# One fused program of a hybrid block and a sparse-attention block on one core: index scores gathered first, the choice of keys spread at one round a step, eight heads computed between projections, rotary angles made in the second feed-forward block

## What is computed

```
q = _rope(_rmsnorm(q, q_norm_g), positions)
k = _rope(_rmsnorm(k, k_norm_g), positions)
qi = _rope(qi, positions)
ki = _rope(_layernorm(ki, idx_k_ln_g, idx_k_ln_b)[:, :, None, :], positions)[:, :, 0, :]
...
s = jnp.einsum('bqhd,bsd->bqhs', qib, ki)
score = jnp.einsum('bqhs,bqh->bqs', jax.nn.relu(s), wib).astype(jnp.float32)
score = jnp.where(causal[None], score, -jnp.inf)
_, sel = lax.top_k(score, topk)
...
logits = jnp.where(sel_ok[:, :, None, None, :], logits, -1e30)
p = jax.nn.softmax(logits, axis=-1).astype(vg.dtype)
```

## Time and profile before

| | |
|---|---|
| median of 3 runs | 2787.43 us (2785.8 to 2787.84) |
| the profiled execution's own time | 2788.58 us |
| its span, first to last instruction | 2786.8 us |
| PE busy | 2720.8 us (98%) |
| DVE busy | 1319.9 us (47%) |
| ACT busy | 929.2 us (33%) |
| POOL busy | 757.6 us (27%) |
| mean granted TensorE clock | 0.986 |
| the sparse mixer up to its output projection | about 1553 to 1821 us of the span |

### The profile page before, as it was taken

One profiled execution on the slowest core, in us unless ns is written; L12 is line 12 of the kernel. 1 busy time (PEld: TensorE's weight loads), 2 busy tenths in 40 slices (PEclk: granted clock), 3 DMA queues, 4 the chain that ended last, 5 costly groups with the idle time before them and its releaser, 6 DMA issues.

```text
span 2786.8 us, 30690 instructions
## 1 busy us (share of the span) xinstructions
PE 2720.8 (98%) x12730; PEld 2190.0 (79%) x12730; DVE 1319.9 (47%) x1846; ACT 929.2 (33%) x1505; POOL 757.6 (27%) x627
## 2 busy tenths in 40 slices
PE   7999999999999999999999998999999999999999
PEld 6888886777777777888888765788888888888887
DVE  4343255555656544634434698463332454633323
ACT  4222233333444332432223433643222332332221
POOL 5574015544555476356700231000000000000000
PEclk9999999999999999999999997999999999999999
DMA  5454234333344255344543110023334323333332
GB/s 170 144 148 126 94 109 120 100 91 91 101 115 113 80 144 157 112 135 141 149 130 115 50 53 25 37 68 99 92 99 135 114 75 92 115 104 99 96 115 77
DMA packets 380763, 294.53 MB, mean 106 GB/s; under 512 B 14804, under 2 KB 334544, under 8 KB 380624
## 3 DMA queue, kind: packets, MB, share of 16 engines
q1 hardware_dynamic: 363632, 240.33, 29.3%
q0 software_dynamic: 16992, 52.25, 6.3%
HBM read 290.40 MB, written 2.13 MB: 105 GB/s over the span
## 4 chain that ended last, share of the span: by engine, by line
PE 86%; DVE 8%; ACT 3%; POOL 1%; DMA 1%; issue 1%; SPq 0%; DVEq 0%; ACTq 0%; POOLq 0%
PE PS L361 17%; PE PS L362 17%; PE PS L364 15%; PE PS L433 7%; PE PS L432 7%; PE PS L431 7%; PE PS L366 2%; PE PS L894 1%; PE PS L398 1%; PE PS L399 1%; PE PS L400 1%; PE PS L867 1%; DVE WL L1509 1%; PE PS L564 1%; DVE SCW L2112 1%; PE PS L589 1%
## 5 line engine op out<-in xcount | busy, mean ns | idle before, releaser
L361 PE MATMUL PS<-HH,WH 128*128 128x512 f32 x2248 | 905.8, 403 | 0.0
L362 PE MATMUL PS<-HL,WH 128*128 128x512 f32 x2248 | 878.1, 391 | 0.0
L364 PE MATMUL PS<-HH,WL 128*128 128x512 f32 x1967 | 769.3, 391 | 0.0
L1509 DVE TENSOR_TENSOR WL<-RAW,WH 128x1024 fp32r<-128x1024 f32 (+1 forms) x306 | 402.1, 1316 | 533.4 <-ACT WH L940 533.2
L361 PEld LDWEIGHTS PS<-HH,WH 128*128 128x128 f32 x2248 | 423.8, 189 | 129.0 <-issue 45.6
L362 PEld LDWEIGHTS PS<-HL,WH 128*128 128x128 f32 x2248 | 424.1, 189 | 90.5 <-issue 6.8
L940 ACT ACTIVATE WH<-RAW 128x1024 fp32r<-128x1024 f32 (+1 forms) x318 | 330.2, 1040 | 367.2 <-PE PS L366 303.1
L364 PEld LDWEIGHTS PS<-HH,WL 128*128 128x128 f32 x1967 | 370.8, 188 | 79.4
L2278 POOL TENSOR_SCALAR ADA<-ADA,CA 128x512 f32<-128x512 f32 x168 | 295.4, 1759 | 10.1 <-DMA ADA<-in_ada_w 2.7
L2275 POOL TENSOR_TENSOR ASUM<-ASUM,ADA 128x512 f32<-128x512 f32 x168 | 230.8, 1374 | 14.0
L431 PE MATMUL PS<-WHr,UH 128*128 128x512 f32 x576 | 224.1, 389 | 0.0
(11 more groups left out here) (335 smaller groups left out, 3361.3 us busy)
## 6 DMA issues: line engine op xcount, KB each, us to landing
ADA<-in_ada_w POOLq DMA_DIRECT2D x192, 256.0 KB, 3.2
RAW<-in_ffn_w_gate SPq DMA_DIRECT2D x88, 512.0 KB, 3.9
RAW<-in_ffn_w_up SPq DMA_DIRECT2D x88, 512.0 KB, 3.9
RAWD<-in_ffn_w_down SPq DMA_DIRECT2D x88, 512.0 KB, 3.5
RAW<-in_w_in SPq DMA_DIRECT2D x84, 512.0 KB, 3.9
RAW<-in_conv_w_in SPq DMA_DIRECT2D x24, 512.0 KB, 3.8
RAW<-in_attn_w_in SPq DMA_DIRECT2D x16, 512.0 KB, 3.8
RAW<-in_w_mlstm_branch SPq DMA_DIRECT2D x8, 512.0 KB, 4.1
```

The source lines that it names most:

```text
L361: pe.matmul(PS[:, b, :], wh[:, k, :], hi[:, k, :], start=k == 0, stop=False)
L362: pe.matmul(PS[:, b, :], wh[:, k, :], lo[:, k, :], start=False, stop=False)
L364: pe.matmul(PS[:, b, :], wl[:, k, :], hi[:, k, :], start=False, stop=False)
L1509: return v.tensor_tensor(out, x, y, op).then_inc(*tick("dve", *event))
```

## The change

1. `indexer` computes the scores of all three blocks one behind the other, each in a buffer of its own (`SC1` to `SC3`). The choice is a generator of its own, `choose`, that runs beside it: one round at each step.
2. Four pairs of heads of token block 0 (`EARLY`, eight heads) are computed by a generator `early` between the chunks of q4 to q7, with buffers `PRE` and `PTE`. The norm factors are made in two halves (`roots`). The loop runs from n = 4.
3. The angles are made by a generator `angles` during the second feed-forward from chunk F2 + 30, their sines by `sines` from F2 + 42; POOL loads the positions earlier.
4. `OB` is swapped: the output of blocks 1 and 3 now lies in banks 0 and 1, that of 0 and 2 in 4 and 7.

```diff
+ANGLES, SINES = F2 + 30, F2 + 42
...
-OB = ((0, 1), (4, 7))
+OB = ((4, 7), (0, 1))
...
+EARLY = 4
...
+def rms_column(tb, c):
+    return 32 * (c // 4) + 8 * tb + 2 * (c % 4)
...
+def prob_part(m, p, e):
+    W = (p // 8 + 1) * P
+    if p < EARLY:
+        return m["PRE"][:, 2 * p + e, :], m["PTE"][:, 2 * p + e, :]
+    return m["F17"][:, (2 * p + e) % 8, 0:W], m["F16"][:, (2 * p + e) % 4, 0:W]
...
+    def choose():
+        for tb in range(1, 4):
+            while ("idx", tb) not in known:
+                yield
             for n in range(16):
-                if n % 2 or at_i["slow"]:
-                    yield
+                yield
             known.add(("mask", tb))
             yield
...
+    def early():
+        while ("q", 3) not in known:
+            yield
+        yield
+        for n in range(EARLY + 2):
+            if n > 1:
+                values(n - 2)
+            if 0 < n <= EARLY:
+                b = yield from behind.bank()
+                clear(b)
+                for e in range(2):
+                    w.wait_ge(*at("exp", n - 1, e))
+                    ins = pe.transpose(PS[:, b, e * P:(e + 1) * P], prob_part(m, n - 1, e)[0], ident)
+                ins.then_inc(*tick("pe", "turned p", n - 1))
+                for e in range(2):
+                    t.mark("pe", "turned p", n - 1, e)
+                free[b] = ("prob read", n - 1, 1)
+            if n < EARLY:
+                scores(n)
+            yield
+            if 0 < n <= EARLY:
+                behind.leave(b)
+            yield
+        known.add("early")
...
+    while ("q", 7) not in known or "early" not in known:
+        behind.step()
+    for n in range(EARLY, 38):
+        if EARLY <= n - 3 < 32:
             values(n - 3)
         if n in OUT_AT:
             out_turned(OUT_AT.index(n))
-        if n >= 2 and n - 2 < 32:
+        if EARLY <= n - 2 < 32:
             turned(n - 2)
         if n < 32:
             while ("mask", pairs[n][0]) not in known:
...
+    def sines():
+        w.wait_ge(*at("angles"))
+        act(m["COS"], m["COS"], ACT.Sin)
+        act(m["SIN"], m["SIN"], ACT.Sin, "cs2")
...
+        if i == SINES:
+            behind.work.append(sines())
...
+    pairs = [(tb, c) for tb in range(4) for c in range(8)]
+    def roots(half):
+        w.wait_ge(*at("rq", 4 * half + 3))
+        cols = slice(32 * half, 32 * half + 32)
+        act(m["RQ"][:, cols], PS[:, 7, cols], ACT.Sqrt, "rq read", half, bias=eps, scale=1.0 / 64.0)
...
-    w.wait_ge(*at("angles"))
-    act(m["CS2"][:, 1, :], m["CS2"][:, 1, :], ACT.Sin)
-    act(m["CS2"][:, 0, :], m["CS2"][:, 0, :], ACT.Sin, "cs2")
...
         low_turned(r, 3)
+    def angles():
+        pf, ang, kr, tmp = (TS[:, 4 + i, :] for i in range(4))
+        w.wait_ge(*at("pos"))
+        copy(pf, m["POSI"][:, :])
+        yield
+        done()
+        ts1(ang, pf, C[:, C_INVF:C_INVF + 1], ALU.mult)
+        yield
...
+        w.wait_ge(*at("sel", 3))
+        done()
+        ts(m["COS"], pf, SIN_MAX, -SIN_MAX, ALU.min, ALU.max)
+        while at_i["chunk"] <= FLUSH[23] + 3:
+            yield
+        w.wait_ge(*at("row", 23))
+        ts(m["SIN"], ang, SIN_MAX, -SIN_MAX, ALU.min, ALU.max, "angles")
...
-    for _ in angle_steps():
-        pass
...
+            known.add(("idx", tb))
+    def choose():
+        for tb in range(1, 4):
+            while ("idx", tb) not in known:
+                yield
+            W, sc = (tb + 1) * P, score_room(tb)
+            wk, src = m["SCW"][:, 0:W], sc
             for n in range(16):
...
-                if n % 2 or at_i["slow"]:
-                    yield
+                yield
...
+    def roots(half):
+        cols = m["RQ"][:, 32 * half:32 * half + 32]
+        w.wait_ge(*at("rq read", half))
+        recip(cols, cols)
+        done()
+        ts1(cols, cols, -0.125, ALU.mult, "rq done", half)
...
-    if ix in behind.work:
-        behind.work.remove(ix)
-    behind.finish()
-    at_i["slow"] = True
-    behind.work.append(ix)
...
+    while ("q", 7) not in known or "early" not in known:
+        behind.step()
+    roots(1)
...
-    ada_sums(5, 24)
+    ada_sums(5, 20)
+    w.wait_ge(*at("y", 2, 3, 1))
+    g.dma_start(m["POSI"][:, :], A["positions_2"][0:1, :].to_broadcast([P, T])).then_inc(*tick("pos", "pos", n=16))
+    ada_sums(20, 24)
...
-    g.dma_start(m["POSI"][:, :], A["positions_2"][0:1, :].to_broadcast([P, T])).then_inc(*tick("pos", "pos", n=16))
...
+            w.wait_ge(*at("angles"))
...
-        over("SCW", [P, 2, T], F32, 47488)
...
+        over("SC1", [P, 2 * P], F32, 43264)
+        over("SC2", [P, 3 * P], F32, 44288)
+        over("SC3", [P, 4 * P], F32, 47488)
+        over("SCW", [P, T], F32, 49536)
+        over("PRE", [P, 8, P], F32, 67968)
+        over("PTE", [P, 8, P], F32, 72064)
```

More of the change, by code:

```diff
@@ L828, in v_tile @@
         held[j] = False
[L830 to L854 removed]
     pairs = [(tb, c) for tb in range(4) for c in range(8)]
[L857 removed]
+    ON, MK, IB = m["F16"], m["MK"], m["IDB"]
     def scores(p):
@@ L1405, in copied, with probs, turned, out_turned @@
         return j
+    pairs = [(tb, c) for tb in range(4) for c in range(8)]
[3 more added lines that the diff above has]
+        act(m["RQ"][:, cols], PS[:, 7, cols], ACT.Sqrt, "rq read", half, bias=eps, scale=1.0 / 64.0)
+    def probs(p):
+        tb, c = pairs[p]
+        for e in range(2):
+            pr = prob_part(m, p, e)[0]
+            w.wait_ge(*at("scored", p, e))
+            act(pr, pr, ACT.Exp, "exp", p, e, bias=least(m, p, e), scale=-1.0, accum_out=total(m, tb, 2 * c + e))
+    def turned(p):
+        W = (pairs[p][0] + 1) * P
+        for e in range(2):
+            w.wait_ge(*at("turned p", p, e))
+            if p > 1:
+                w.wait_ge(*at("values", p - 2, e))
+            act(prob_part(m, p, e)[1], PS[:, 5 + e, 0:W], ACT.Copy, "prob read", p, e)
+    def out_turned(tb):
+        for h in range(2):
+            w.wait_ge(*at("out turned", tb, h))
+            act(m["OH"][:, 4 * h:4 * h + 4, tb * P:(tb + 1) * P],
+                PS[:, OB[tb % 2][h], :].rearrange("p (k t) -> p k t", t=P), ACT.Copy, "o hi", tb, h)
+    def early():
+        yield
+        roots(0)
+        while ("q", 3) not in known:
+            yield
+        yield
+        for n in range(EARLY + 2):
+            if 0 < n <= EARLY:
+                b = yield from behind.bank()
+                w.wait_ge(*at("turned p", n - 1))
+                act(m["PTE"][:, 2 * n - 2:2 * n, :], PS[:, b, 0:2 * P].rearrange("p (e t) -> p e t", e=2), ACT.Copy,
+                    "prob read", n - 1, 1)
+                t.mark("act", "prob read", n - 1, 0)
+            if n < EARLY:
+                probs(n)
+            yield
+            if 0 < n <= EARLY:
+                behind.leave(b)
+            yield
+        known.add("early")
     w.wait_ge(*at("ada sum", 23))
@@ L1425, in scalar_program @@
         behind.work.append(rope(j, ("qi", c)))
-    ix = indexer()
-    behind.work.append(ix)
+    behind.work.append(indexer())
+    behind.work.append(choose())
     for c in range(2):
@@ L1439, in scalar_program @@
             behind.work.append(g)
[L1440 to L1474 removed]
+            if (key, c) == ("q", 3):
+                behind.work.append(early())
+    while ("q", 7) not in known or "early" not in known:
+        behind.step()
+    roots(1)
+    for n in range(EARLY, 38):
+        if EARLY <= n - 2 < 32:
             turned(n - 2)
@@ L1566, in fm @@
         flush_due(i)
+        if i == ANGLES:
+            behind.work.append(angles())
         return i
@@ L2105, in indexer, with choose @@
             tt(sc[:, W - P:W], sc[:, W - P:W], tri, ALU.add)
-            src = sc
+            known.add(("idx", tb))
+    def choose():
+        for tb in range(1, 4):
+            while ("idx", tb) not in known:
+                yield
+            W, sc = (tb + 1) * P, score_room(tb)
+            wk, src = m["SCW"][:, 0:W], sc
             for n in range(16):
@@ L2227, in out_low, with early @@
                      m["OH"][:, 4 * h:4 * h + 4, tb * P:(tb + 1) * P], ("o hi", tb, h), "o", tb, h)
-    for n in range(38):
+    def early():
+        yield
+        roots(0)
+        while ("q", 3) not in known:
+            yield
+        yield
+        for n in range(EARLY + 2):
+            if 0 < n <= EARLY:
+                b = yield from behind.bank()
+            if n < EARLY:
+                probs(n)
+            yield
+            if 0 < n <= EARLY:
+                behind.leave(b)
+            yield
+        known.add("early")
+    j = take_x()
+    first_qi = take_x()
+    behind.work.append(index_key(j))
+    for c in range(4):
+        if c > 1:
+            side_fm()
+        j = take_x() if c else first_qi
+        behind.work.append(rope(j, QI[:, c, :], ("qi", c)))
+    behind.work.append(indexer())
+    behind.work.append(choose())
+    for c in range(2):
+        side_fm()
+        behind.work.append(v_tile(c, take_x()))
+    for tile, n in ((k_tile, 2), (q_tile, 8)):
```

(12 more changed lines are left out.)

200 lines of the change are left out of this document (66 added, 134 removed).

## The result

The changed kernel takes 2791.86 us in the median of 18 runs (2788.72 to 2795.34), the kernel before 2787.35 (18 runs). The ratio is 1.0017, with a 95% interval of 1.0010 to 1.0024: 4.5 us slower, or 0.17%. That is a loss, though a small one; a gain of 6.9 was forecast. The profiled execution has a span of 2792.5 us and an own time of 2794.31. Of all kernels here, three executions ran at a low clock throughout and took over 600 us longer; they are left out of every median and ratio.

The account below looks back on a forecast made before the run. VectorE's list was taken to bound the stretch from block 1's scores to the loop's first probabilities. -1.3 + 1.5 - 8.1 + 1.0 = -6.9 us gave 2781.7, as a median 2780.5; the 8 in 10 range was 2771.5 to 2791.

Parts of the forecast that it names:

- A: Index key chain: with the angles moved to the second feed-forward, a ScalarE table load goes, -1.3 us (0 to -2.2).
- B: From block 1's scores to the loop's first probabilities: a shorter VectorE list against new waits between engines, +1.5 us.
- list: VectorE's work from block 1's scores to the loop's first probabilities: 104.5 us, 2.4 less than before.
- coupling: Same stretch, early pairs: VectorE and TensorE wait for each other each chunk, so VectorE cannot run ahead, +3.9 us.
- the coupling case: Rival on the early pairs' waits: B at +6 to +8, C at -7, sum about -1.5, 2786 us; chance 0.25.
- C: The loop up to `probs(14)`, now begun at pair 4: 30.8 us instead of 38.9, so -8.1 us.
- D: Hand-over to `down`: with `OB` swapped, the first product waits for an output copy from bank 0, +1.0 us.
- slower: Rival: TensorE falls to 1.2 GHz through q5 to q7, total +13, about 2801 us; chance 0.13.

Follow-up runs that it names:

- e8: The changed kernel with ScalarE's exponentials of an early pair, and the transposes and values behind them, issued one turn later; 2783.46 us, ratio 0.9986.
- e3: The changed kernel with VectorE's probabilities of an early pair ahead of the choice round of the same step instead of behind it; 2794.96 us, ratio 1.0026.
- e10: The changed kernel with three steps between early pairs instead of two; 2796.68 us, ratio 1.0035.
- e5: The kernel before with only the angles moved into the second feed-forward; 2785.93 us, ratio 1.0000.
- e9: The kernel of e8 with the first four products of `down` in the order of banks 2, 0, 1, 3; 2782.42 us, ratio 0.9984.

## Why the prediction was wrong

**The bound** was read rightly: VectorE's list sets the end of the stretch. In e1, without early pairs, the stretch is as long as before, and TensorE's idle time only gathers in front of the loop (12.56 us).

**A, -1.3 forecast, -0.5 found.** The table load did leave the chain. But the square root then waits for a product of TensorE, 0.81 us (it starts at 1574.04 in the changed kernel), so only the rest of the 1.28 was won. The feed-forward lost nothing, as forecast (from 1350 to 1510 us TensorE is busy throughout at clock 1.00). On the two loads ahead of the loop, the Trainium skill, page "ScalarE: Activation LUTs", section "What ACT_TABLE_LOAD costs", gives a drain of 1.38 us more for each; ScalarE's timeline shows none:

```profile
1714.08 0.60 ACT L985 ACTIVATE TS<-PS 128x512 f32<-128x512 f32 x1
1714.69 1.28 ACT L985 ACT_TABLE_LOAD   x1
1715.99 0.29 ACT L985 ACTIVATE RQ<-PS,C 128x32 f32<-128x32 f32 x1
1716.29 1.28 ACT L985 ACT_TABLE_LOAD   x1
```

The copy ends at 1714.68, and square root and loads follow one another within 0.02 us. By these rows the trace does not agree, and the sum rightly went by 1.28.

**B, +1.5 forecast, +13.6 found: this is the step that failed.** It had two terms, a list and a coupling.

The list was put at 104.5 us with no wait left in it; without its waits it is 107.2 in the changed kernel (120.4 less 13.2) and 105.6 in e8 (111.0 less 5.3). So 2.7 us of the 12.1 that are missing lie in the list. VectorE rows that grow beside GpSimd's (last section), which the sum left as they were, are 3.5 us more than before and cover it. Another 2.0 us are a wait for a copy of the index heads: the prediction took all 4.0 us of those out, reading them as waits at the start of a block's heads, but the two largest of the three (2.07 and 1.08 us) stood at the last two heads of block 3, and the changed kernel has a new one of 2.02 us at the first head of block 2.

The coupling is what failed most, by 7.3 us (11.2 of waits for early scores against 3.9): "that VectorE cannot run ahead I price at +3.9" came from comparing what a chunk costs TensorE with what it costs VectorE, as if the two only had to keep pace. Each wait was bounded by the largest one seen, 1.44 us.

But here the hand-over to a late engine cost its lateness, and that lateness was in the rows: TensorE waited 5.06 us for VectorE ahead of the loop. The scores of pair 0 met 8 us of it. It went on to TensorE since the next chunk's copies stood behind the exponential in ScalarE's order, and it came back to VectorE as 7.16 and 4.04 us of dry waiting, as TensorE reached the next scores a chunk later, at half clock.

The prediction named this order ("VectorE's copy of the same step may stand behind a round") and gave it 6 to 8 us and a chance of 0.25; e3 shows that the round in the same step was 1.2 us of it, and e8 that the place in ScalarE's order was the larger part (7.9 us of VectorE's waits gone, TensorE's wait of 9.12 down to 4.43). The sum of that rival, "about -1.5", is the one for B at +6; with B at +8 its own terms give +0.7.

**C, -8.1 forecast, -8.1 found.** The mechanism is right: the mask falls in front of pair 14 and TensorE waits 2.47 us (3 forecast). That the number agrees so well is luck. The three parts took 9.0, 13.7 and 8.1 us where 8.8, 12.8 and 7.5 were forecast, 1.7 us more in sum, and this stands in place of the 1.7 us for the clock behind the wait, which was counted in C but falls behind `probs(14)`, where 1.2 is seen. (By the parts given, the bounds of C come to 27.0 and 33.6, not 27.3 and 33.9.) The same loop took 28.3 us in e3 and 32.1 in e10, and its length before was 37.3 in e5 instead of 38.9.

**D, +1.0 forecast, 1.0 found for the wait, and 1.0 to 1.3 more behind it.** The first product starts 1.70 us after the last transpose group (1828.25 and 1826.55) instead of 0.72, as forecast. The extra is the longer time at the low level: 1.3 us to the fifth product, and the whole place 2.1 us longer than before, 2.0 in e8 against e9. The prediction put it at nothing.

The case "slower" had TensorE's clock as its mechanism, with 54 us for 27 us of work. The clock did fall, to 0.50 to 0.60 from 1675 to 1690 us, but it fell within the wait of 9.12 us; over the stretch it is 0.90, as before (0.91). What the fall cost in the stretch was not measured apart. The mechanism of the loss was that of the coupling case, with B at +13.6 where it had +6 to +8, and this was enough to turn the gain into a loss.

## What to carry over

From this case: when work is moved so that engines depend on each other both ways, price the first hand-over at the lateness of the late engine at that moment, then look at what is queued behind the waiting instruction on each engine in between; the next engine's wait is that one too. Issue a stage's result to the in-order engine only behind the work that others want now: one turn of delay was worth 8 us here. Rounds of a bound engine were free only in places where the other engine had work of its own. And a sum that agrees to 0.1 us (C here) is worth taking apart before it is called right.

## What the hardware showed unexpectedly

A VectorE instruction of 0.36 us took 2.49. It is the mask of block 2 in the changed kernel:

```profile
1707.78 2.49 DVE L1590 TENSOR_SCALAR MK<-TS 128x384 bf16<-128x384 f32 x1
```

GpSimd's subtraction had begun 0.10 us earlier:

```profile
1707.68 2.38 POOL L2383 TENSOR_TENSOR WLr<-RAWD,WHr 128x1024 fp32r<-128x1024 f32 x1 [6.15 <-ACT WHr L985]
```

VectorE's instruction ends 0.2 us after GpSimd's; without such a neighbour it takes 0.36 (the kernel before has it at 1680.09). It isn't the only one. Another, of 0.29 us elsewhere, begins 0.23 us behind a subtraction:

```profile
1658.33 2.30 DVE L1587 TENSOR_TENSOR SC<-SC,C 128x128 f32<-128x128 f32 x1
```

In the stretch of the changed kernel eight rows of VectorE took over 0.2 us more than the shortest row of the same operation and shape in these traces, 11.5 us in all, and each of them overlaps a row of GpSimd. Before there are six such rows, 8.0 us in all, and in e8 eight, 9.9 us. So by this count 3.5 us of the longer stretch are rows that meet GpSimd's differently in the new order, and 1.6 us of what e8 gives back; seven of the eight rows stand ahead of `probs(0)` and belong to VectorE's lateness there. How late VectorE would be with nothing on GpSimd beside it was not tested.

The trace agrees with the Trainium skill, page "SBUF — State Buffer", section "SBUF: two separate sides", where the port pair of the two engines is a lock that one of them holds for a whole instruction. That these instructions are of the kind that takes the lock was not tested apart.
